# Last stage of a fused decoder step: the prompt's gate row and scale row stay in PSUM, and the gated sum is written to PSUM

## The reference, cut to what matters

```python
    x = x + (gt2[:, None, :] * ff.astype(jnp.float32)).astype(x.dtype)     # end of _block
    ...
    shp, scp = _adaln(c_prompt, w_ada_final, b_ada_final, 2)
    y_prompt = _norm_modulate(xp, g_final, shp, scp)                       # the same for the sample rows

def _norm_modulate(x, g, shift, scale):
    h = _rmsnorm(x, g) * (1.0 + scale[:, None, :]) + shift[:, None, :]
```

## Time and profile before

| | us |
|---|---|
| median of 3 runs | 2283.53 |
| the 3 runs | 2263.2, 2283.53, 2288.75 |
| the profiled execution's own time | 2278.31 |
| its span (first to last instruction) | 2276.5 |
| last stage of it: first transpose (2209.91) to the end | 66.6 |

### The profile page before, as it was taken

The page is one execution under the profiler, slowest core; times in us unless marked ns, Lnnn a source line. Parts: engine busy times, 40 slices in busy tenths (PEclk is TensorE's granted clock), DMA queues, the critical chain, the costliest instruction groups (busy, mean ns, idle before and its releaser), DMA issues.

```text
span 2276.5 us, 28877 instructions
## 1 busy us (share of the span) xinstructions
PE 2005.9 (88%) x8246; PEld 1052.2 (46%) x8247; DVE 889.3 (39%) x2410; ACT 509.0 (22%) x933; POOL 396.4 (17%) x345
## 2 busy tenths in 40 slices
PE   4797899998887989889889999998999999998980
PEld 1456555444552435464344544454455545543450
DVE  2826500135873222235323333333333333332338
ACT  3422210005771110232111111111111111111122
POOL 0010000004552030000011221212122222211214
PEclk7898889998998899988989999999999999999995
DMA  9641200010104520021278998998988797898853
GB/s 337 244 157 24 117 0 0 1 74 9 39 2 136 180 102 0 29 92 52 100 283 271 298 301 286 305 287 281 298 259 251 205 300 248 270 298 268 274 122 126
DMA packets 100878, 394.20 MB, mean 173 GB/s; under 512 B 27279, under 2 KB 30003, under 8 KB 71996
## 3 DMA queue, kind: packets, MB, share of 16 engines
q1 hardware_dynamic: 70020, 302.44, 35.8%
q0 software_dynamic: 24768, 90.19, 16.6%
q10 hardware_dynamic: 6024, 0.73, 0.3%
HBM read 329.16 MB, written 62.57 MB: 172 GB/s over the span
## 4 chain that ended last, share of the span: by engine, by line
PE 29%; DMA 23%; issue 6%; SPq 4%; DVE 3%; ACT 1%; POOL 0%; POOLq 0%; DVEq 0%; ACTq 0%
DMA arena<-in_w_exp_down 23%; PE psum L992 11%; PE psum L1020 6%; PE psum L862 5%; SPq L2277 2%; PE psum L978 1%; SPq L2273 1%; SPq L2272 1%; DVE arena L1642 1%; PE psum L889 1%; PE psum L841 1%; PE psum L895 1%; DVE arena L1652 1%; PE psum L902 0%; PE psum L885 0%
## 5 line engine op out<-in xcount | busy, mean ns | idle before, releaser
L992 PE MATMUL psum<-arena 128*128 x1360 | 626.8, 615 | 48.8 <-SPq L2298 42.7
L992 PEld LDWEIGHTS psum<-arena 128*128 128x128 f32 x1360 | 259.3, 196 | 349.1 <-issue 349.1
L1020 PE MATMUL psum<-arena,tail 128*128 x672 | 302.3, 592 | 0.0
L2125 POOL DMA_INDIRECT moe_rows<-arena x84 | 133.4, 1588 | 803.6 <-ACT arena L1976 264.8
L1598 DVE TENSOR_TENSOR arena<-arena,psum 128x256 f32<-128x256 f32 x85 | 35.8, 421 | 488.2 <-ACT arena L1962 488.2
L1020 PEld LDWEIGHTS psum<-arena,tail 128*128 128x128 f32 x672 | 121.1, 190 | 120.5 <-issue 120.5
L1962 ACT ACTIVATE arena<-psum 128x256 f32<-128x256 f32 x85 | 32.6, 384 | 633.0 <-PE psum L992 633.0
L689 PE MATMUL psum<-arena 128*128 128x512 f32 (+1 forms) x384 | 126.7, 493 | 0.0
L862 PE MATMUL psum<-arena 128*128 128x512 f32 (+1 forms) x288 | 124.4, 593 | 0.3 <-ACT arena L1879 0.3
L1576 DVE TENSOR_TENSOR arena<-tail,arena 128x1152 bf16<-128x1152 f32 x89 | 119.6, 1344 | 0.0
L1976 ACT ACTIVATE arena<-psum,arena 128x512 f32<-128x512 f32 x84 | 57.7, 687 | 213.4 <-PE psum L1020 208.2
(11 more groups left out here) (492 smaller groups left out, 2378.0 us busy)
## 6 DMA issues: line engine op xcount, KB each, us to landing
arena<-in_w_exp_gate SPq DMA_DIRECT2D x64, 1024.0 KB, 5.3
arena<-in_w_exp_up SPq DMA_DIRECT2D x64, 1024.0 KB, 9.1
arena<-in_w_exp_down SPq DMA_DIRECT2D x64, 1024.0 KB, 12.2
arena<-in_w_ada SPq DMA_DIRECT2D x24, 1024.0 KB, 7.8
arena<-in_w_ada_final SPq DMA_DIRECT2D x8, 1024.0 KB, 6.5
arena<-in_cache_k SPq DMA_DIRECT2D x32, 256.0 KB, 3.4
arena<-in_cache_v SPq DMA_DIRECT2D x32, 256.0 KB, 2.9
arena<-in_w_in SPq DMA_DIRECT2D x1, 6176.0 KB, 18.5
```

The costliest lines, as they stand in the source:

```text
L992: ins = pe.matmul(slot[2 + par].rearrange("p (h n) -> p h n", h=2), xTs[:, par, k, :], ring_gu[:, at, :, k, :].rearrange("p a h n -> p (a ...
L1020: ins = pe.matmul(slot[1][:, n * 512:(n + 1) * 512], hTs[:, k, :], ring_d[:, at, k, n, :].rearrange("p a n -> p (a n)"), start=(k == 0), s ...
L2125: pool.indirect_dma_start(y_dram, bass.IndirectOffsetOnAxis(ap=s_idx[:, par:par + 1], axis=0), y_buf[:, par, :], None, compute_op=ALU.add) ...
```

## The change

The prompt's gate row (q = 0) and its row a (q = 1) are written by TensorE into `slot[0]` and `slot[1]` first, under the key "FP", and are never copied: VectorE reads them there for tiles 0 to 7. The four other row sets (`FIN_ROWS`: prompt shift, then the sample's gate, a and shift) still go to `fin_rows`, but through the one-bank slots in halves of 512: sets 0 and 2 through `slot[2]` and `slot[3]`, sets 1 and 3 through `slot[4]` and `slot[5]`. The product y * gate is no longer written over `y_rows` but to PSUM, to banks 4 and 5 for even tiles and 6 and 7 for odd ones, that is over `slot[2]` to `slot[5]`; VectorE's first two products wait until ScalarE has drained these. VectorE waits for `rows_ready` only at tile 8, and GpSimd now waits for it before its first add.

```diff
+        FIN_ROWS = ((2, 0), (0, 1), (1, 1), (2, 1))
...
-            for q, (c, src) in enumerate(((40, mod_t), (0, af), (48, mod_t))):
-                for smp in range(2):
-                    fill(pe, ("FR", q, smp), smp)
-                    for k in range(KD):
-                        s_ = fin_s_cols[:, q, k, :] if smp else src[:, c + k, 0:1].to_broadcast([P, P])
-                        ins = pe.transpose(slot[smp][0:NS if smp else P, k * P:(k + 1) * P], s_, ident)
-                    full(ins, ("FR", q, smp))
+            fin_cols = ((40, mod_t), (0, af), (48, mod_t))
+            for q in range(2):
+                c, src = fin_cols[q]
+                fill(pe, ("FP", q), q)
+                for k in range(KD):
+                    ins = pe.transpose(slot[q][:, k * P:(k + 1) * P], src[:, c + k, 0:1].to_broadcast([P, P]), ident)
+                full(ins, ("FP", q))
+            for i, (q, smp) in enumerate(FIN_ROWS):
+                c, src = fin_cols[q]
+                for n in range(2):
+                    s_ = 2 + 2 * (i % 2) + n
+                    fill(pe, ("FR", i, n), s_)
+                    for k in range(4):
+                        col = fin_s_cols[:, q, 4 * n + k, :] if smp else src[:, c + 4 * n + k, 0:1].to_broadcast([P, P])
+                        ins = pe.transpose(slot[s_][0:NS if smp else P, k * P:(k + 1) * P], col, ident)
+                    full(ins, ("FR", i, n))
...
-            dve.wait_ge(rows_ready, 1)
+            full(dve, ("FP", 0))
+            full(dve, ("FP", 1))
             for t in range(NT + 2):
                 if t < NT:
-                    m, s_ = rows(t), int(t == 8)
+                    m = rows(t)
                     dve.wait_ge(ld_row[t], 32)
-                    dlink(tt(y_rows[0:m, t, :], y_rows[0:m, t, :], fin_rows[0:m, s_, :], ALU.mult))
-                    tt(x1[0:m, t, :], x1[0:m, t, :], y_rows[0:m, t, :], ALU.add).then_inc(x2_ready, 1)
+                    gated = psum[0:m, 4 + 2 * (t % 2):6 + 2 * (t % 2), :].rearrange("p a b -> p (a b)")
+                    if t < 2:
+                        slots.wait_empty(dve, ("FR", 2 + t, 0))
+                        slots.wait_empty(dve, ("FR", 2 + t, 1))
+                    if t == 8:
+                        dve.wait_ge(rows_ready, 1)
+                    dlink(tt(gated, y_rows[0:m, t, :], slot[0] if t < 8 else fin_rows[0:m, 1, :], ALU.mult))
+                    tt(x1[0:m, t, :], x1[0:m, t, :], gated, ALU.add).then_inc(x2_ready, 1)
...
-                    stt(x1[0:m, i, :], x1[0:m, i, :], rstd[0:m, i:i + 1], fin_rows[0:m, 2 + s_, :], ALU.mult, ALU.mult).then_inc(y_scaled, 1)
+                    stt(x1[0:m, i, :], x1[0:m, i, :], rstd[0:m, i:i + 1], fin_rows[0:m, 3, :] if s_ else slot[1], ALU.mult, ALU.mult).then_inc(y_scaled, 1)
...
-            for q in range(3):
-                for smp in range(2):
-                    full(act, ("FR", q, smp))
-                    m = NS if smp else P
-                    empty(f(fin_rows[0:m, 2 * q + smp, :], slot[smp][0:m, :], ACT.Copy), ("FR", q, smp))
+            for i, (q, smp) in enumerate(FIN_ROWS):
+                m = NS if smp else P
+                for n in range(2):
+                    full(act, ("FR", i, n))
+                    empty(f(fin_rows[0:m, 2 * q + smp, n * 512:(n + 1) * 512], slot[2 + 2 * (i % 2) + n][0:m, :], ACT.Copy), ("FR", i, n))
...
+                if t == 0:
+                    pool.wait_ge(rows_ready, 1)
                 pool.wait_ge(y_scaled, t + 1)
```

More of the change, by code:

```diff
@@ L1978, in _ @@
             act.wait_ge(weights_in, E)
-            for q in range(3):
-                for smp in range(2):
-                    full(act, ("FR", q, smp))
-                    m = NS if smp else P
-                    empty(f(fin_rows[0:m, 2 * q + smp, :], slot[smp][0:m, :], ACT.Copy), ("FR", q, smp))
-            slots.wait_empty(act, ("FR", 2, 1))
-            slots.wait_empty(act, ("FR", 2, 0))
+            for i, (q, smp) in enumerate(FIN_ROWS):
[3 more added lines that the diff above has]
+                    empty(f(fin_rows[0:m, 2 * q + smp, n * 512:(n + 1) * 512], slot[2 + 2 * (i % 2) + n][0:m, :], ACT.Copy), ("FR", i, n))
+            for i in (2, 3):
+                for n in range(2):
+                    slots.wait_empty(act, ("FR", i, n))
             act.sem_inc(rows_ready, 1)
```

## The result

Twelve runs of each kernel: the change has a median of 2262.59 us (2253.87 to 2274.53), the kernel before 2283.32 (2263.2 to 2292.22). The ratio of the means is 0.992 (that of the medians 0.991) with a 95% interval of 0.9892 to 0.9949, that is 12 to 25 us less. Forecast were 2268.5 us and a gain of 15.0. The profiled execution took 2257.94 us with a span of 2256.2.

A forecast was written before the change was run, and what follows sets the result against it. VectorE was taken to bound the last 66.6 us, taking turns with GpSimd. Gains of 12.1 (steady tiles), 1.6 (start) and 1.3 (end) sum to 15.0 us, 0.66%: median forecast 2268.5 us, range 2251 to 2284.

The forecast's parts named there:

- The steady tiles: Last stage, sums of tiles 3 to 8: each takes 1.22 us in place of 3.24, gaining 12.1 us.
- Rival 1: Steady tiles: VectorE and GpSimd still take turns, not because of the second SBUF input; only 1.6 us won, 2282 us; 8%.
- the rule: VectorE beside GpSimd's add: an instruction with one SBUF input, or none, passes without waiting.
- The small TENSOR_SCALAR on 128x1: Steady tiles, L1646 near the end of GpSimd's add: 0 to 0.6 us over six tiles if held; taken as 0.
- Reading and writing PSUM: VectorE instructions of the last stage: PSUM access costs 0 us more than SBUF; 8.6 us kept for the range.
- Rivals 2, 3 and 4: Product passes PSUM twice, 8.6 us (8%); fixed price per PSUM input, 0.5 us (6%); slow VectorE PSUM writes, 2297 us (3%).
- The product of tile 8: Last tile, two SBUF inputs kept: it starts before GpSimd's add, which waits and shows 3.25 us.
- The start: First transpose to first product of the last stage: product starts 1.6 us sooner, range 0.9 to 2.0.
- (b): First product waits for y_rows of tile 0, landing 3.8 us after issue at the earliest, at 2217.2.
- (c): First product waits until banks 4 and 5 are drained by ScalarE's six half copies, at 2217.3 to 2217.8.
- The end: End of tile 6's scaling to GpSimd's last end: about 8.1 us in place of 9.4, gaining 1.3; 2.4 if not held.
- The sign that did come: Prediction is wrong if the time before the last stage moves by more than a few us.

The follow-up runs named there:

- e1: Kernel before with only the product y * gate written to PSUM and read there by the sum; 2281.4 us in one run, last stage 57.7 us.
- e2: The change with the product back over y_rows in SBUF, only gate row and row a in PSUM; 2273.52 us in one run, last stage 59.6 us.
- e3: Kernel before without GpSimd's shift add, which only signals; 2264.19 us in one run, last stage 47.5 us.
- e4: Kernel before with GpSimd's shift add replaced by a memset of unused SBUF; 2275.03 us in one run, last stage 51.8 us.
- e7: The change with the prompt's gate row back in SBUF, product and row a still in PSUM; 2270.82 us in one run, last stage 52.2 us.
- e6: The change run again, unedited; median 2274.79 us over 10 runs, ratio 0.9928 to the kernel before, last stage 51.45 us.
- e5: The change with the sample's a and shift in PSUM and VectorE adding tile 8's shift; median 2269.56 us, ratio 0.9919 to the kernel before.
- e8: The change with y_rows loads of tiles 2 to 8 issued only after tile 0 landed; 2262.52 us in one run, last stage 51.5 us.
- e9: Kernel before with GpSimd's shift add replaced by adding constant 0, reading one SBUF tensor; 2276.2 us in one run, last stage 58.1 us.

## Why the prediction was right

**The steady tiles** (12.1 us forecast). From product to product of tiles 3 to 8 the change takes 2240.59 - 2221.37 = 19.22 us in place of 29.34, 10.1 less, and the sum of tile 8 another 2.0: 12.1. That it is the second SBUF input of a VectorE instruction beside a reading GpSimd instruction is shown by e1, e2, e3, e4 and e7, each of which moves operands of one kind or one engine's instruction. Rival 1 is out: the halves do what they should, and e4 gives full overlap with both engines on SBUF. A small slip: a tile's 5.87 us are VectorE's 3.85 and 2.02 of waiting, not GpSimd's 2.2; the sum ends 1.07 us after GpSimd's add and takes 1.22 undisturbed, so the two overlap by 0.15.

**What the earlier trace rows was read to say.** The prediction takes from these rows that an instruction with one SBUF input passes. The held instruction there, L1371, has itself only one SBUF tensor as input; the rest is a factor per partition and a constant (`ts(new_mask, iota_row[0:NS, 0:CH], att_one[0:NS, 8:9], NEG, ALU.is_gt, ALU.mult)`). And eight equal copies of 64x64 elements from SBUF to SBUF, which stand beside the same GpSimd adds in the kernel before, differ by a factor of six:

```profile
L1376 DVE COPY arena<-arena x8: 192/497/1155, 687.2 to 691.9; 64x64 f32<-64x64 f32 x8
```

So the rule is too wide. For TENSOR_TENSOR and SCALAR_TENSOR_TENSOR it holds, by the change, e1 and e7, and these are all the large VectorE instructions of this stage. The small TENSOR_SCALAR on 128x1, for which the prediction took 0 of 0 to 0.6 us, passes too: 0.14 us at 2240.45 in e7, where the add runs until 2241.48. That the term came out does not rest on the rule as it was worded, and which copies and TENSOR_SCALAR forms wait beside a GpSimd add was not tried.

**Reading and writing PSUM** (0 us). 1222 ns for the product, 1220 for the sum, 1281 for the scaling, against 1224 and 1284 in SBUF. Rivals 2, 3 and 4 are out. The Trainium skill (VectorE: DVE Perf Modes, section The TRN2 errata) has 120 fixed cycles from PSUM against 58 from SBUF, by estimate 65 ns more for each of the instructions with a PSUM input. There are 25 of these, not the 27 of the prediction, and nothing of the 65 ns is seen in them.

**The product of tile 8** went first and GpSimd's add waited, 3.26 us, without a cost at the end, as said.

**The start** (1.6 us forecast, 0.9 to 2.0) failed in the first profile: 0.25 us were lost. The step that failed is (b), the landing of y_rows: I took its least time of one profile, 3.8 us, for the time, and it was 5.6. In e6, where it was 3.9, the start is 7.62 us, a gain of 1.6 against the one profile of the kernel before. Nor did the step that the prediction let decide, (c), decide anywhere: in the first profile and in e5, e6 and e8 the first product waits for the load. In e6 the sixth of the eight half copies ended, by estimate from 3.97 us for eight, at 7.1 us after the first transpose, where 7.5 were forecast. That 1.6 came out in e6 is in part luck. With the row copies as before (before, e1, e3, e4, e9) the start is 8.8 to 9.3, with those of the change (e2, e6, e8 and the first profile) 7.6 to 9.5.

**The end** (1.3 us forecast): 9.4 became 8.0, 1.4. VectorE went first, one of the two orders given.

**The sum.** 13.3 us in the first profile and 15.1 in e6, against 15.0, both measured from the single profile of the kernel before. The medians differ by 20.7 us; what goes beyond the stage's share has no cause in the change that any profile shows. The median came out at 2262.59 where 2268.5 was forecast; the 6 us lie within the runs' own spread, and the second set of ten runs has its median at 2274.79, on the other side. The ratios, 0.992 and 0.9928, and the forecast 0.9934 agree within their intervals. So the 15.0 us are borne out by the stage, and how near the median came is chance.

**The sign that did come.** The prediction was to be wrong if the time before the last stage moved by more than a few us. It moved by 7.1 us in the first profile and by 13.9 the other way in e6. The sign was a bad one and says nothing on the mechanism: the same kernel scatters there by 21.0 us, and three runs of the kernel before, known beforehand, already lay 25.6 apart.

## What to carry to other kernels

Where GpSimd and VectorE work in one stage, compare an instruction's longest time with its shortest: a sum at 3.24 us with a minimum of 1.22 waits while it shows as busy, and a busy share of 99% hides it. For a VectorE instruction with two tensor inputs, one input moved to PSUM, the output of the instruction before it included, takes it out of the way at no cost of its own (copies and TENSOR_SCALAR are another matter, see the earlier trace rows above); which of the inputs matters is read from who is running when each instruction is issued, all the way round the loop, since an add that is delayed by one instruction runs into the next. Of such a change the steady part can be forecast to a tenth of a microsecond, while a start that waits for a DMA's landing can't be from one profile.

## What the runs showed of the hardware that I had not expected

- A GpSimd memset of 2.23 us in SBUF runs fully beside VectorE instructions with two SBUF inputs (e4), so GpSimd's writes alone hold nothing.
- A GpSimd add of a constant holds VectorE's sum for 0.7 us only, of its own 2.76 (e9), while a two-tensor add of 2.34 holds it nearly to its end: the sum ends 1.08 us later (e2), of 1.22 that it takes.
- VectorE reads and writes PSUM in one instruction at the same 1.22 us per 1,024 columns as it reads one operand there.
- An instruction of VectorE that stands waiting goes ahead of GpSimd's next one, though that is ready at the same moment (the change's end, 2246.92, and once each in e2, e6, e7 and e8, where the last scaling shows 1.96 us).
